# Prompt attention of a hybrid decoder: products with the values once per two steps, without a pass of zeros

## The reference, cut to what matters

```python
DILATED_GROUPS = ((128, 1), (512, 4), (2048, 16))
...
    s = jnp.einsum('brnqhc,brnkhc->brnhqk', qg, kb) * scale
    s = jnp.where(mask[None], s, NEG_INF)
    m = jnp.max(s, axis=-1, keepdims=True)
    p = jnp.exp(s - m)
    den = jnp.sum(p, axis=-1)
    o = jnp.einsum('brnhqk,brnkhc->brnqhc', p, vb) / den_t[..., None]
```

## Time and profile before

| | |
|---|---|
| median of 3 runs | 1900.48 us (1899.53 to 1900.77) |
| profiled execution, its own time | 1899.82 us |
| its span | 1898.0 us |
| TensorE busy | 1858.3 us, 98% of the span |
| VectorE, ScalarE, GpSimd busy | 1205.3, 708.7, 662.2 us |
| prompt attention, from S0 to the next product | 738.7 to 863.7 us of the span |

### The profile page before, as it was taken

How to read it: one execution, slowest core, us unless ns; L and a number is a source line. 1 busy time by engine, 2 the same in 40 slices (tenths; PEclk the granted TensorE clock), 3 DMA queues, 4 the chain that set the end, 5 groups by cost and what they waited for, 6 DMA issues and landing times.

```text
span 1898.0 us, 35890 instructions
## 1 busy us (share of the span) xinstructions
PE 1858.3 (98%) x15190; PEld 1771.3 (93%) x15190; DVE 1205.3 (64%) x1512; ACT 708.7 (37%) x944; POOL 662.2 (35%) x338
## 2 busy tenths in 40 slices
PE   8999999999999999999999999999999999999997
PEld 8999999989889897678999999899999999999996
DVE  8899652255444645673445746885555675878988
ACT  6311222244443445663200034523444445333332
POOL 0122111212111113443466641137777761432504
PEclk9999999999999999999999999999999999999998
DMA  5422533866676753732354332433334466656333
GB/s 176 116 90 80 138 113 114 251 205 198 217 229 203 235 160 121 206 117 102 125 181 148 131 122 77 157 144 114 137 125 157 162 217 248 202 196 194 117 134 138
DMA packets 191415, 298.73 MB, mean 157 GB/s; under 512 B 37248, under 2 KB 133248, under 8 KB 187680
## 3 DMA queue, kind: packets, MB, share of 16 engines
q1 hardware_dynamic: 184352, 270.60, 44.5%
q10 hardware_dynamic: 6912, 25.96, 3.4%
HBM read 215.12 MB, written 79.28 MB: 155 GB/s over the span
## 4 chain that ended last, share of the span: by engine, by line
PE 84%; DVE 8%; DMA 3%; issue 2%; POOL 2%; ACT 1%; SPq 0%; POOLq 0%; DVEq 0%; ACTq 0%
PE ps L2644 37%; PE ps L3176 26%; PE ps L3020 3%; PE ps L2984 2%; PE ps L3110 2%; PE ps L2904 1%; PE ps L2817 1%; PE ps L3096 1%; PE ps L2659 1%; PE ps L2798 1%; PE ps L2874 1%; PE ps L2913 1%; DMA w_raw<-in_w 1%; PE ps L2779 1%; PE ps L2946 1%
## 5 line engine op out<-in xcount | busy, mean ns | idle before, releaser
L1161 POOL TENSOR_TENSOR w_lo<-w_raw,w_hi 128x1024 fp32r<-128x1024 f32 x48 | 121.1, 2524 | 620.7 <-ACT w_hi L1310 620.7
L2644 PE MATMUL ps<-op_hi,w_hi 128*128 128x352 f32 x1392 | 309.0, 330 | 0.1
L2644 PE MATMUL ps<-op_lo,w_hi 128*128 128x352 f32 x1392 | 301.8, 325 | 0.0
L2644 PE MATMUL ps<-op_hi,w_lo 128*128 128x352 f32 x1392 | 300.2, 323 | 0.0
L2644 PEld LDWEIGHTS ps<-op_hi,w_hi 128*128 128x128 f32 x1392 | 233.5, 188 | 15.2 <-issue 13.2
L2644 PEld LDWEIGHTS ps<-op_lo,w_hi 128*128 128x128 f32 x1392 | 237.5, 188 | 0.0
L2644 PEld LDWEIGHTS ps<-op_hi,w_lo 128*128 128x128 f32 x1392 | 236.8, 188 | 0.0
L1384 ACT ACTIVATE stage<-ps 128x1056 f32<-128x1056 f32 x48 | 50.5, 1052 | 280.7 <-PE ps L2644 280.7
L1168 POOL TENSOR_TENSOR w_hi<-w_raw,zeros 128x1024 fp32r<-128x1024 f32 x24 | 62.0, 2583 | 171.1 <-PE ps L3110 63.0
L3176 PE MATMUL ps<-do_hi,w_hi 128*128 128x264 f32 x560 | 114.0, 285 | 1.7 <-DVE w_lo L2470 1.0
L3176 PE MATMUL ps<-do_lo,w_hi 128*128 128x264 f32 x560 | 113.2, 284 | 0.0
(11 more groups left out here) (477 smaller groups left out, 4598.7 us busy)
## 6 DMA issues: line engine op xcount, KB each, us to landing
w_raw<-in_w SPq DMA_DIRECT2D x101, 512.0 KB, 4.2
t_raw<-tmp_h SPq DMA_DIRECT2D x28, 1056.0 KB, 5.7
kc<-in_k_cache SPq DMA_DIRECT2D x48, 448.0 KB, 5.1
vc<-in_v_cache SPq DMA_DIRECT2D x48, 448.0 KB, 6.0
out_keep<-stage ACTq DMA_DIRECT2D x24, 528.0 KB, 2.7
tmp_gate_d<-stage ACTq DMA_DIRECT2D x24, 528.0 KB, 4.7
gate_t<-tmp_gate_d SPq DMA_DIRECT2D x24, 528.0 KB, 3.6
tmp_h<-o_t SPq DMA_DIRECT2D x18, 528.0 KB, 3.1
```

The source lines that it names most:

```text
L1161: pool.tensor_tensor(lo, w_raw[:, b], hi.bitcast(F32), ALU.subtract).then_inc(w_split[b], 1)
L2644: mm = pe.matmul(ps[:, 3 * dst + q, 0:BLK], w[:, b, w0 + n], x[:, k, q * BLK:(q + 1) * BLK], start=(n == 0 and part == 0), stop=(n == len( ...
```

## The change

TensorE takes the steps in twos: S and T of one step, S and T of the next, and then N and F of the two steps before, and one count of `at_pv` for both. The zeros are gone: the first matmul into each bank has `start=True`. The near products go by query tile (blocks `q` and `q - 1` into tile `q`), 128 columns each. V moves to the odd steps (`V_STEPS`: steps 1, 9, 15, 23, 29). VectorE copies the outputs out later (`2 * visits(...) + 2`; the first half of the last pair at step 41), and the far keys are made after step 3 of a pair. The waits for `at_pv` are counted anew.

```diff
-V_STEP = 1
+V_STEPS = [PER * _w + 1 + _w % 2 for _w in range(HP - 1)]
...
+LAST_USE = [3, 3, 3, 3, 5, 5, 6]
+def visits(g):
+    return g // 2 + 1
...
# far_values, both at_values
-                    sy.wait_ge(at_pv, PER * (w - 1))
+                    sy.wait_ge(at_pv, visits(PER * (w - 1) - 1))
...
# GpSimd
-                if g % PER == PER - 3 and w < HP:
+                if g % PER == PER - 4 and w < HP:
...
# at_copy on ScalarE and VectorE
-                wait(act, at_pv, g - g % PER - 1)
+                if g >= PER:
+                    act.wait_ge(at_pv, visits(g - g % PER - PER + LAST_USE[g % PER]))
...
# VectorE
-                if g % PER == 4:
-                    at_outputs(g // PER, 7)
-                if g % PER == 0 and g:
-                    at_outputs(g // PER - 1, 6)
+                for w in range(HP):
+                    if g == min(2 * visits(PER * w + 3) + 2, NG - 1):
+                        at_outputs(w, 7)
+                    if g == 2 * visits(PER * w + PER - 1) + 2:
+                        at_outputs(w, 6)
...
# TensorE
-            def near_block(w, j, uses):
+            def near_block(w, j, q, b, opens=False, closes=False):
                 for a, rows in enumerate(heads):
-                    at_block = [8 * max(x - 1, 0) + 4 * a + b for x, b in uses]
-                    got = pt_blocks[:, at_block[0]:at_block[-1] + 1:at_block[-1] - at_block[0] if n > 1 else 1]
-                    mm = pe.matmul(ps[rows, 6 + q // 4, P * (q % 4):P * (q % 4 + n)].rearrange("p (q n) -> p q n", q=n),
-                                   vn[:, w % 2, j, rows], got, start=False, stop=(j == 1))
+                    mm = pe.matmul(ps[rows, 6 + q // 4, P * (q % 4):P * (q % 4 + 1)], vn[:, w % 2, j, rows],
+                                   pt_blocks[:, 8 * max(q - 1, 0) + 4 * a + b], start=opens, stop=closes)
...
-                    pe.matmul(ps[:, 7 - s // 4, :], zeros[:, 0:P].bitcast(F32R), zeros[:].bitcast(F32R), start=True, stop=False)
...
+                for q in STEP_TILES[s]:
+                    mm = near_block(w, q, q, 2 if q == 1 else q > 0, opens=q in (7, 3))
+                    if q:
+                        mm = near_block(w, q - 1, q, int(q == 1), closes=q == 1 and w % 2 == 0)
...
-            for g in range(NG + 1):
-                if g + AHEAD < NG:
-                    at_scores(g + AHEAD)
-                if g < NG:
-                    at_transposes(g)
+            for g in range(0, NG, 2):
+                for x in (g, g + 1):
+                    if x + AHEAD < NG:
+                        at_scores(x + AHEAD)
+                    at_transposes(x)
                 if g:
-                    at_outputs(g - 1)
-                if g % PER == V_STEP and g // PER + 1 < HP:
-                    at_values(g // PER + 1)
+                    at_outputs(g - 2)
+                if g + 1 in V_STEPS:
+                    at_values((g + 1) // PER + 1)
+            at_outputs(NG - 2)
```

More of the change, by code:

```diff
@@ L161 @@
     GRAN += 2
-    if _g % PER == V_STEP and _g // PER + 1 < HP:
+    if _g in V_STEPS:
         V_GRAN[_g // PER + 1] = [GRAN, GRAN + 1]
         GRAN += 2
+LAST_USE = [3, 3, 3, 3, 5, 5, 6]
+def visits(g):
+    return g // 2 + 1
 def members(g):
@@ L1486, in at_values @@
                 if w >= 2:
-                    act.wait_ge(at_pv, PER * (w - 1))
+                    act.wait_ge(at_pv, visits(PER * (w - 1) - 1))
                 s.activation(vn[:, w % 2, 0:4].rearrange("p j m -> p (j m)"), ps[:, 4, :], ACT.Copy).then_inc(at_even, 1)
@@ L1504, in _ @@
                 at_copy(g)
-                if g % PER == V_STEP and g // PER + 1 < HP:
+                if g in V_STEPS:
                     at_values(g // PER + 1)
@@ L2162, in at_copy @@
                 dve.wait_ge(at_t, P_GRAN[g][1] + 1)
-                wait(dve, at_pv, g - g % PER - 1)
+                if g >= PER:
+                    dve.wait_ge(at_pv, visits(g - g % PER - PER + LAST_USE[g % PER]))
                 v.tensor_copy(pt[:, q - 1, 1, 0:n].rearrange("p j m -> p (j m)"), ps[:, 5, 0:n * P]).then_inc(at_odd, 1)
@@ L2169, in at_values @@
                 if w >= 2:
-                    dve.wait_ge(at_pv, PER * (w - 1))
+                    dve.wait_ge(at_pv, visits(PER * (w - 1) - 1))
                 v.tensor_copy(vn[:, w % 2, 4:8].rearrange("p j m -> p (j m)"), ps[:, 5, :]).then_inc(at_odd, 1)
             def at_outputs(w, bank):
-                dve.wait_ge(at_pv, PER * w + (4 if bank == 7 else PER))
+                dve.wait_ge(at_pv, visits(PER * w + (3 if bank == 7 else PER - 1)))
                 wait(dve, yo_out[w % 2], 16 * (w // 2))
@@ L2905, in at_transposes @@
                     mm.then_inc(at_t, 1)
-            def near_block(w, j, uses):
-                q, n = uses[0][0], len(uses)
+            def near_block(w, j, q, b, opens=False, closes=False):
                 for a, rows in enumerate(heads):
-                    at_block = [8 * max(x - 1, 0) + 4 * a + b for x, b in uses]
-                    got = pt_blocks[:, at_block[0]:at_block[-1] + 1:at_block[-1] - at_block[0] if n > 1 else 1]
-                    mm = pe.matmul(ps[rows, 6 + q // 4, P * (q % 4):P * (q % 4 + n)].rearrange("p (q n) -> p q n", q=n),
-                                   vn[:, w % 2, j, rows], got, start=False, stop=(j == 1))
+                    mm = pe.matmul(ps[rows, 6 + q // 4, P * (q % 4):P * (q % 4 + 1)], vn[:, w % 2, j, rows],
+                                   pt_blocks[:, 8 * max(q - 1, 0) + 4 * a + b], start=opens, stop=closes)
                 return mm
@@ L2921, in at_near @@
                 if g == 0:
-                    te.wait_ge(w_zero, 1)
                     te.wait_ge(sa_o, ROUNDS)
-                if w and s in (0, 4):
-                    te.wait_ge(at_o, 2 * w - 1 + (s == 4))
                 if s in (0, 4):
-                    pe.matmul(ps[:, 7 - s // 4, :], zeros[:, 0:P].bitcast(F32R), zeros[:].bitcast(F32R), start=True, stop=False)
[L2928 to L2934, removed]
+                    wait(te, at_o, 2 * w - 1 + (s == 4))
+                for q in STEP_TILES[s]:
+                    mm = near_block(w, q, q, 2 if q == 1 else q > 0, opens=q in (7, 3))
+                    if q:
+                        mm = near_block(w, q - 1, q, int(q == 1), closes=q == 1 and w % 2 == 0)
                 return mm
@@ L2947, in at_far, with at_outputs @@
                                            start=False,
-                                           stop=(c == 1 and x == RES - 1))
+                                           stop=((c == 1 if s == 3 else w % 2 == 1) and x == RES - 1))
                 return mm
[L2951 to L2954, removed]
+            def at_outputs(first):
+                for g in (first, first + 1):
+                    mm = at_near(g)
+                for g in (first, first + 1):
+                    if g % PER in (3, 5):
+                        mm = at_far(g)
                 mm.then_inc(at_pv, 1)
```

## The result

The changed kernel takes 1905.31 us (median; 1901.01 to 1908.96) against 1900.53 for the kernel before (1897.37 to 1906.03). The ratio, taken from executions run side by side, is 1.0021, 95% interval 1.0013 to 1.0028: slower by 4.0 us, between 2.5 and 5.3. I had said 1900.2, in 1895.0 to 1904.5, and had given "slower" 0.18.

What follows compares the result with a forecast made beforehand. TensorE's order of passes was taken to bound the middle of the stage; savings, two load waits of 2.6 us and an end costing 0.5 more summed to +0.1 us, hence 1900.2 us, range 1895.0 to 1904.5.

Steps and rivals of the forecast that it cites:

- The split costs nothing: Near matmuls cut to 128 columns: same columns in 144 more pieces, taken to add no time.
- the pairing: Steps taken in twos on TensorE: 42 groups of products become 21, 0.155 us saved each, 3.3 us in all.
- V4 waits for nothing: V4 lies 19.7 us behind S20 and its loads come 18.4 behind, so it has no wait.
- The queue: SyncE's late output store delays pair 3's loads to 18.1 us behind S14; V3 waits 2.6 us, V5 as long.
- To S40: Stage from S14 to S40: zeros save 1.7 us, groups 2.0; S40 at 843.3 without the waits of V3 and V5.
- with two waits of 2.6 at 848.5: S40's forecast start once the waits of V3 and V5 for loads, 2.6 us each, are added to 843.3.
- At the full clock: Finding on the kernel before: TensorE busy without a gap from 780 to 850 us at full clock.
- my own bound of 4.0: Upper bound on V3's wait for loads: slowest landings, 4.4 and 8.9 us, give 19.5 behind S14.
- The loads are in time: Rival: value store and third load take their lower bounds, V3 and V5 don't wait; 5.2 us less, 1895.0; chance 0.25.
- The copies bound each block: Rival: VectorE's copy reaches the second T 0.4 us late in 20 blocks, 8.0 us partly hidden; 1905.5; chance 0.13.
- The split costs its turns: Rival: 36 added near blocks cost up to 0.155 us each, partly hidden at V3 and V5; 1903.5; chance 0.07.

Runs made afterwards that it cites:

- `fill_three`: The changed kernel with transposes of ident, results unread, ahead of the waits of V2 (10), V3 and V5 (24 each); 1901.09 us, ratio 1.0006.
- the turned queue: The changed kernel with SyncE's store of a pair's output issued behind the next pair's values and loads; 1898.24 us, ratio 0.9983.
- `split_no_zeros`: The kernel before with near products by query tile, 128 columns each, start flags for the zeros, old order of steps; 1899.68 us, ratio 1.0002.
- `pair_only_3`: The changed kernel with SyncE's store behind the loads, but the zeros and 256-column value blocks of the kernel before; 1899.9 us, ratio 1.0006.
- the old kernel with the turned queue: The kernel before with SyncE's store issued one turn later, behind the next pair's loads; 1901.09 us, ratio 1.0005.

## Why the prediction was wrong

**Which terms held.** Up to the start of V3 the sum came out within a tenth, 53.67 behind S0 against 53.58. That closeness is in part luck: S14 started 0.6 sooner behind S0 than forecast, V3 0.7 later behind S14 (18.82 against 18.1), and the other two profiles have V3 at 51.75 and 54.80. The chain of the queue, on which I had said all depends, has its parts in the trace: copy of the outputs done 3.85 behind S14 (4.0 forecast), values issued 0.53 later (0.4), landing in 4.2 (3.6), loads issued 9.95 behind S14 (8.9), the last of them landing in 7.8 (8.2). The split costs nothing, four blocks take 1.02, the pairing is worth 0.145 for each pair of steps by the profiles, and V4 waits for nothing, or 0.70. V5 to k3 without a fall of the clock takes 37.63, against a forecast of 37.9: V5 to S40 16.2 and S40 to k3 21.4, where my terms give 16.2 and 21.7.

**The step that failed** stands under "The queue" and is carried into "To S40": "with two waits of 2.6 at 848.5". I priced each wait at its own length and let TensorE go on behind it at the pace of the earlier trace rows. "At the full clock" stood in my first paragraph as a finding about the kernel before. That it might end where the change makes TensorE stand idle was no term of the sum, no bound and no rival. The trace of before seemed to bear me out, as it has a wait of 1.62 at V2 with the clock at 1.00 behind it; the new waits were to be half as long again (2.6), and no row there covered that. The first profile has them nearly twice as long, 3.17 and 2.95.

| | forecast | first profile |
|---|---|---|
| S0 to V3 | 53.6 | 53.67 |
| V3 to V4 | 20.7 | 22.44 (20.91 where the clock stayed) |
| V4 to V5 | 19.3 | 19.61 |
| V5 to k3 | 37.9 | 39.20 (37.63 where the clock stayed) |
| stage | 131.5 | 134.92 |

The first and the last figure of the forecast are in the prediction. Between them, V3 to V4 is V (1.02) and the 19.7 behind S20. V3 to V5 is the 39.43 of the kernel before, less four zeros and seven groups (2.04), with a wait of 2.6: 40.0. The rest is V5 to k3.

The clock is 1.5 and 1.6 of the 3.4 us between the two sums. The mean stage of the three profiles is 3.6 above the forecast, and of this the falls are 2.7 (3.1, 1.5 and 3.5 in the three). A second term was also too small: the waits of V3 and V5, 5.2 together by my sum, were 6.0 to 6.1, and the 4.44 of V5 in the third lies above my own bound of 4.0. `fill_three` shows that the clock is a cost of its own and not another name for the wait: the waits stayed, the clock stayed up, and 2.9 us went.

**The rivals.** "The loads are in time" did not happen in any of three profiles of the changed kernel; it is what the turned queue makes true. The stage is then 126.17, where I had worked out 131.5 - 5.2 = 126.3; the time was 1898.2, not 1895.0. "The copies bound each block" fell: V1 to V2, which has no wait for a load in the second profile, takes 20.91, and no second T waits for VectorE in the middle of the stage. Its number, 1905.5, is nearly the one measured; that is luck, as the mechanism is another. "The split costs its turns" fell with `split_no_zeros`.

**The range.** It reached up to 1904.5, by the waits' own bounds of up to 4.0 and the rivals. With a fall of the clock behind each wait as a bound, the forecast's own upper end would have been 1903.0 + 3.1 = 1906.1, and the measured time inside.

**Outside the stage** the span differs by more than the change can reach: 1766.6 us in the profile before, 1770.6 to 1771.5 in three profiles of the changed kernel, 1765.6 to 1771.0 in nine other kernels. In part this is the clock too. TensorE waits 1.18 us near the end of every execution; in 11 of the 13 profiles the clock falls behind that wait, and not in those of the kernel before and `pair_only_3`. From the end of that wait to the end of the span the latter two take 34.9, the others 36.3 to 36.5, and 37.9 where the clock stays low for longer. In the changed kernel's first profile:

```profile
1869.51 0.32 PE L3122 MATMUL ps<-ones,pre_rstd 128*88 128x1 f32 x2 [1.18 <-DVE stage L2583]
```

```profile
1871.00:1875.00 4.00, 4.00 (x23) 4.00 (x22) 1.63 (x5) 1.57 (x4) 0.00 (x0) 0.58 0.46 184
```

Another part is a wait of TensorE for GpSimd's `w_lo` near 1110 us, which takes from 1.28 to 3.14, with a fall behind it in 4 of the 13. Why the wait changes, and the rest of the scatter, stay open. As the old kernel with the turned queue has both falls as well (1770.1), I don't put them down to the change. Differences of less than about 3 us between single profiled executions are not to be read without the stage's own rows.

## What to carry to other kernels

Price a new wait of TensorE at more than its length: ask for the clock behind it, and keep a second figure for the passes that follow (here 1.5 to 1.6 us, and once 2.0). When an engine's copy is moved back, look at what stands behind its reader in an in-order queue: here a store that nobody needed soon held up the loads that everybody needed, and one edit that puts the store behind them turned a loss of 4.0 us into a gain of 3.2. A saving of TensorE's passes paid here only where the next transfers kept the faster pace.

## What the runs showed of the hardware that was not expected

- In the rows behind V3 TensorE's clock is still 1.00 when it begins to work again, falls to 0.50 some 1.4 us later and comes back 3.5 us after that. At V5 it fell 0.35 us behind the start in the first profile, and 2.3 us before it in the third. The Trainium skill, TensorE: Matmul & The Clock Gate, HAM oscillation, describes a TensorE that waits for transfers between bursts of products and starts the next burst at the lower clock. The trace agrees that the clock falls around such waits, with 1.5 to 2.0 us lost for each; that the work starts at the lower clock it shows only at V5 of the third profile.
- The length of the wait alone doesn't tell whether it falls. In the stage it fell behind waits of 2.95, 3.17, 3.50 and 4.44, and not behind 2.53, 2.10, 1.64 or 1.58; but twice it fell at V2, behind 1.30 and 1.12 with 0.68 for `far_k` soon after, where 1.64 and 0.68 in another kernel left it at 1.00. Outside the stage it fell in 11 of 13 executions behind a wait of 1.18, and not behind waits of 3.14 and 3.03 for `w_lo`.
- The waits of V3 in the three executions of the changed kernel, 3.17, 2.53 and 1.58, do not come from slower or faster loads. From the issue of the first load of pair 3 to V3 it takes 8.9, 8.5 and 8.9. The loads leave 44.8, 43.2 and 45.9 behind S0, and TensorE is ready for V3 at 50.5, 49.2 and 53.2.
